# The first products of each SwiGLU stage on the tile of tokens that is ready first, the other tile's rows turned between them, and an MLP that waits for its hidden tiles in fours

## The chip, the cores and the metric

The kernel runs on one core of a Trainium2 chip. The metric is device time in microseconds of one execution, inputs and outputs in the chip's memory, all numbers fp32. Lower is better.

## What is computed

Two blocks of two layers each work on 256 tokens of width 1024. The first block (a diffusion-like block with attention, retention and an S5 scan) also has 256 context tokens in its first layer. What the change touches are its two MLPs and the four SwiGLU layers of the second block:

```python
def squared_relu_mlp(h, w1, w2):
    return jnp.square(jax.nn.relu(h @ w1)) @ w2

def swiglu(x, w_gate, w_up, w_down):
    return (jax.nn.silu(x @ w_gate) * (x @ w_up)) @ w_down

def second_block(x, ...):
    for l in range(DEPTH):
        x = layer_norm(ALPHA * x + 0.5 * swiglu(x, ffn1_w_gate[l], ffn1_w_up[l], ffn1_w_down[l]), ln1_g[l], ln1_b[l])
        y = hybrid_mixer(x, w_in[l], ...)
        x = layer_norm(ALPHA * x + y, ln2_g[l], ln2_b[l])
        x = layer_norm(ALPHA * x + 0.5 * swiglu(x, ffn2_w_gate[l], ffn2_w_up[l], ffn2_w_down[l]), ln3_g[l], ln3_b[l])
    return x
```

`w_gate` and `w_up` are 1024 x 2816, `w_down` 2816 x 1024.

## The kernel before

Each engine has its own program, written out by hand in the order in which it runs; the engines meet at semaphores. Tokens lie in tiles of 128 (t = 0 and 1; in MLP0, the first layer's MLP, also two context tiles). Weights are streamed by the SP queue into a ring of four slots; the load of a slot is released when TensorE has begun the weight tile after the one that was in it (`mm` with `T.first`), so the place of that matmul in TensorE's order sets when the load is issued.

**MLP0** (`tensor_mlp0`, `vector_mlp0`) goes over the hidden width in two halves. A half makes 16 hidden tiles f of 128 columns for 512 tokens on TensorE, VectorE squares the relu of each into `h1T` (L866, L868), then the second product runs for two column halves s, in four parts of four f each, over four token tiles. Between these products TensorE does pieces of the S5 preparation: transposes L2034 of the "ends" that VectorE has built (`ends_built`, its marker copy L2015) and the lags (L2049). VectorE computes S5 powers and levels behind f = 12 and f = 14. Ahead of the second product TensorE waits for `hidden_ready`, which VectorE raises by a marker copy (L887) after f = 15.

**A SwiGLU stage** (`tensor_ffn`, `scalar_ffn`, `vector_ffn`; stage n = 0 to 3) goes over w_gate and w_up in 11 groups ("units") of 256 columns. The product of two token tiles with gate and up over two halves of the depth is made in seven products of four matmuls instead of eight (a fast matrix scheme): products 0 and 1 are plain ones (tile 0 with the gate), the others take sums: `token_sum` (four, L2722, 512 columns) and `weight_sum` (four per unit, L2735, 1024 columns), all made by VectorE. VectorE adds the products up (L2767), ScalarE takes silu, VectorE multiplies (L2772), TensorE turns the hidden rows, ScalarE copies them. The down product (`tensor_seven`) has the same scheme for 768 columns; the last 256 columns are plain products, tile by tile (`tensor_last_columns`), 22 matmuls each (32 in the MLP of the second layer, MLP1).

**Between stages** each row tile gets its last sums (`vector_last_rows` after a SwiGLU stage: L2634; `vector_sum` after a mixer: L2823; L2873 and L2876 after MLP1), its norm (`vector_norm_tile`, L2840, with a root on ScalarE), is turned by TensorE (`tensor_turn_rows`, L2434, eight transposes) and copied with the norm's gain and shift to the columns `hT` (`drain_rows_turned`, on ScalarE L2452, on VectorE L2454). Only when both tiles' columns are there (`tensor_needs_hT`) does TensorE begin stage n, and VectorE its token sums and weight sums (`vector_ffn_sums`), followed by the rows for the next residual (`vector_next_rows`, L2849 to L2855: six operations). Stages 0 and 2 follow MLP1 and the layer before, where tile 0 is ready first; stages 1 and 3 follow a mixer, whose output product does tile 1 first. The mixers (`tensor_mixer2`) turn tile 0 first and begin with products on it.

## Time and profile before

| | |
|---|---|
| median of 3 runs | 2543.18 us (2539.36 to 2544.16) |
| the profiled execution, whole | 2542.72 us |
| its span in the profile | 2540.9 us |
| busy: TensorE, VectorE, ScalarE, GpSimd | 92%, 53%, 16%, 8% |
| mean granted clock of TensorE | 0.964 of 2.4 GHz |
| chain that ended last | PE 82%, DVE 11%, DMA 3%, ACT 2% |

The span is one profiled execution; the time of that execution contains 1.8 us around it. PE is TensorE, DVE VectorE, ACT ScalarE, POOL GpSimd, SPq the queue that loads weights. In a timeline a row merges instructions of one kind that follow one another, and its bracket gives the idle time of the engine in front of it and the instruction that ended it. Each fp32 matmul stands as two records.

### The profile page before, as it was taken

Reading aid. Unit: us, or ns where it says so; the run is one execution under the profiler, and the core shown is the slowest. Engines: PE = TensorE matmul, PEld = TensorE weight load, DVE = VectorE, ACT = ScalarE, POOL = GpSimd, SP = SyncE. Lnnn points to the kernel's source line nnn. Section 1 sums busy time; section 2 is a strip of 40 time slices with the busy share of each in tenths; the row PEclk is TensorE's granted clock in tenths of the full one; section 3 lists DMA queues with packets and bytes.
Section 4 is the critical chain, followed back from the end, with each engine's and each line's share of the span. In section 5 each row is a group of like instructions: output and inputs, shape, how many; then the busy total and the mean of one; then the engine's idle time right before and its main releaser. Section 6 shows DMA issues by size and latency. Waiting matters only on the chain.

```text
span 2540.9 us, 28736 instructions
## 1 busy us (share of the span) xinstructions
PE 2343.4 (92%) x11250; PEld 1553.0 (61%) x11250; DVE 1338.2 (53%) x2596; ACT 417.7 (16%) x913; POOL 205.5 (8%) x396
## 2 busy tenths in 40 slices
PE   7999989999999985499999999889999999889998
PEld 3445654444444433258768866557867886566885
DVE  2145563265566027424547763248766874255875
ACT  2122342000101013320001100131101110131110
POOL 1000000302555201000001000000000000000000
PEclk9999999999999997699999999899999999999999
DMA  7547612423444318245446554415555555514553
GB/s 244 190 151 240 202 49 66 102 66 108 149 150 149 124 58 291 101 132 152 154 158 219 167 159 143 126 47 164 171 161 159 170 164 161 147 50 141 170 162 124
DMA packets 278087, 371.10 MB, mean 146 GB/s; under 512 B 24838, under 2 KB 231169, under 8 KB 273217
## 3 DMA queue, kind: packets, MB, share of 16 engines
q1 hardware_dynamic: 260432, 332.30, 41.0%
q0 software_dynamic: 16752, 36.44, 4.6%
q8 instruction: 90, 1.47, 0.3%
q10 hardware_dynamic: 768, 0.53, 0.1%
q14 instruction: 45, 0.36, 0.0%
HBM read 345.10 MB, written 22.02 MB: 144 GB/s over the span
## 4 chain that ended last, share of the span: by engine, by line
PE 82%; DVE 11%; DMA 3%; ACT 2%; issue 1%; SPq 0%; POOL 0%; DVEq 0%; ACTq 0%; POOLq 0%
PE banks L222 72%; DMA weights<-in_w_in 1%; DMA weights<-in_ada_w 1%; PE banks L1338 1%; PE banks L1367 1%; DVE big L2735 1%; PE banks L2660 1%; PE banks L449 1%; PE banks L3257 1%; PE banks L3230 1%; PE banks L2034 0%; ACT h_columns L2452 0%; PE banks L1356 0%; DVE normed_rows L1632 0%; ACT normed_rows L3344 0%
## 5 line engine op out<-in xcount | busy, mean ns | idle before, releaser
L222 PE MATMUL banks<-weights,big 128*128 128x256 f32 (+4 forms) x2128 | 581.5, 445 | 70.1 <-ACT big L1036 51.0
L222 PE MATMUL banks<-weights,h_columns 128*128 128x256 f32 (+4 forms) x1664 | 544.1, 483 | 26.5 <-DVEq L2459 8.0
L222 PEld LDWEIGHTS banks<-weights,big 128*128 128x128 f32 (+2 forms) x2128 | 342.4, 187 | 272.7 <-issue 143.1
L222 PEld LDWEIGHTS banks<-weights,h_columns 128*128 128x128 f32 x1664 | 322.6, 196 | 221.8 <-issue 150.2
L222 PE MATMUL banks<-h_columns,weights 128*128 128x512 f32 (+1 forms) x1024 | 338.4, 491 | 4.2 <-ACTq L2459 2.4
L222 PEld LDWEIGHTS banks<-h_columns,weights 128*128 128x128 f32 x1024 | 195.2, 192 | 133.5 <-issue 117.1
L222 PE MATMUL banks<-big 128*128 128x256 f32 x1056 | 235.5, 379 | 2.2 <-DVE big L2735 2.2
L222 PEld LDWEIGHTS banks<-big 128*128 128x128 f32 x1056 | 200.3, 190 | 30.9 <-DVE big L2735 3.4
L2767 DVE TENSOR_TENSOR big<-banks,big 128x256 f32<-128x256 f32 x308 | 130.1, 422 | 85.1 <-PE banks L222 79.3
L2100 POOL DMA_DIRECT2D s_inside<-kernel_lags x256 | 127.4, 506 | 47.3 <-ACT statistics L2084 44.7
L2578 DVE TENSOR_TENSOR normed_rows<-weights 128x384 f32<-128x384 f32 x120 | 66.9, 558 | 101.0 <-PE banks L222 98.7
L222 PE MATMUL banks<-normed_rows,big 128*128 128x384 f32 (+1 forms) x368 | 115.6, 449 | 0.0
L2808 POOL DMA_DIRECT2D row_vectors<-in_ln_g x6 | 3.3, 544 | 1346.9 <-DVE statistics L2855 804.3
L2735 DVE TENSOR_TENSOR big<-weights 128x1024 f32<-128x1024 f32 x88 | 107.8, 1225 | 5.9 <-DMA weights<-in_ffn_w_up 3.0
L2735 DVE TENSOR_TENSOR big<-weights,big 128x1024 f32<-128x1024 f32 x88 | 107.8, 1225 | 3.0
L222 PEld LDWEIGHTS banks<-normed_rows,big 128*128 128x128 f32 (+1 forms) x368 | 59.4, 176 | 40.6 <-DVE normed_rows L2578 0.6
L222 PE MATMUL banks<-big,h_columns 128*128 128x256 f32 x352 | 83.3, 379 | 0.0
L721 DVE TENSOR_TENSOR normed_rows<-banks,row_vectors 128x512 f32<-128x512 f32 x16 | 11.1, 692 | 131.5 <-PE banks L222 131.3
L866 DVE TENSOR_SCALAR normed_rows<-banks 128x512 f32<-128x512 f32 x32 | 22.1, 691 | 101.5 <-PE banks L222 101.0
L1036 DVE COPY big<-banks 128x512 f32<-128x512 f32 (+5 forms) x50 | 31.4, 628 | 75.5 <-PE banks L222 64.5
L222 PE MATMUL banks<-weights,silu_c 128*32 128x256 f32 x768 | 52.1, 413 | 18.7 <-DMA weights<-in_ada_w 13.9
L2578 DVE TENSOR_TENSOR normed_rows<-weights,normed_rows 128x384 f32<-128x384 f32 x120 | 67.0, 558 | 4.2
(468 smaller groups left out, 2296.9 us busy)
## 6 DMA issues: line engine op xcount, KB each, us to landing
weights<-in_mlp_w SPq DMA_DIRECT2D x52, 1024.0 KB, 5.4
weights<-in_ada_w SPq DMA_DIRECT2D x48, 1024.0 KB, 7.3
weights<-in_ffn_w_gate SPq DMA_DIRECT2D x44, 1024.0 KB, 5.3
weights<-in_ffn_w_up SPq DMA_DIRECT2D x44, 1024.0 KB, 5.3
weights<-in_ffn_w_down SPq DMA_DIRECT2D x48, 768.0 KB, 4.3
weights<-in_w_out SPq DMA_DIRECT2D x12, 1024.0 KB, 5.0
weights<-in_mlp_w SPq DMA_DIRECT2D x16, 768.0 KB, 4.3
weights<-in_w_in SPq DMA_DIRECT2D x16, 768.0 KB, 4.5
```

The lines of the kernel that those rows point to most:

```text
L222: ins = T.engine.matmul(out, lhsT, rhs, start=start, stop=stop)
L449: ins = T.engine.matmul(self.ps[:, bank, 2 * j:2 * j + 2], self.ada_rows[:, n % 2 if buffer is None else buffer, j * P:(j + 1) * P], self. ...
L1036: return (lane.engine.copy if lane.name == "scalar" else lane.engine.tensor_copy)(out, in_)
L1338: ins = e.matmul(self.ps[:, n % 2, c0:TOK], self.qkT[0:QK, h % 2, 0, t * P:(t + 1) * P], self.qkT[0:QK, h % 2, 1, c0:TOK], start=True, sto ...
L1367: ins = e.matmul(self.ps[o:o + V_DIM, b, 0:P], self.kv[:, u, h, NOPE:NOPE + V_DIM], self.pT_of(m)[:, u * P:(u + 1) * P], start=u == keys[0 ...
L2100: e.dma_start(dst, src).then_inc(self.sem("inside_stored"), 16)
L2578: V.engine.tensor_tensor(out, in0, in1, ALU.subtract).then_inc(self.sem("down_sums"), 1)
L2660: ins = T.engine.transpose(self.ps[:, 7, f * N_LAT + t * P:f * N_LAT + (t + 1) * P], self.hidden_rows[:, t, f * P:(f + 1) * P], self.ident ...
L2735: V.engine.tensor_tensor(out, in0, in1, ALU.subtract).then_inc(self.sem("weight_sums"), 1)
L2767: e.tensor_tensor(out, self.ps[:, b, 0:256], other, ALU.add).then_inc(self.sem(name), 1)
L3230: ins = e.matmul(out, self.zT[:, h0 + j, t * P:(t + 1) * P], self.zT[:, 12 + g:16:2, 0:keys], start=True, stop=True)
L3257: ins = e.matmul(self.ps[:, 6 + m % 2, o:o + HD + 1], self.pT2[:, m % 2, j, 2 * c + u, :], self.v2[:, u, c, g, :], start=u == 0, stop=u == t)
```

## The change

- **MLP0.** The marker copy `hidden_ready` is gone. Each hidden tile raises `hidden_tiles`, and TensorE waits, in the first column half, for four more of them ahead of each of the four parts.
- **The turning of the first tile.** It stands inside the second tile's last product: after two of the weight tiles of `tensor_last_columns` (six matmuls of 22 are left, 16 of 32 in MLP1), or between the two column halves of the mixer's output product. The mixer's entry has it too.
- **The SwiGLU stage.** In stages 1 and 3 the roles of the tiles are swapped (`ffn_tile`), so that the plain products 0 and 1 of the first unit are on the tile turned first. They wait for that tile's columns alone (`first_columns`, raised by ScalarE). The other tile is turned behind product 0 (stages 0 and 2) or behind product 1 (stages 1 and 3).
- **VectorE.** The first unit's weight sums 0 and 1 stand ahead of the second tile's last sums instead of behind the token sums (`vector_first_weight_sums`); in stage 0 they lie in other memory. At the mixer's entry VectorE copies tile 0's turned half before it takes up tile 1.

```diff
@@ tensor_mlp1, tensor_mlp0
-        self.tensor_last_columns(T, self.mlp1_down())
+        self.tensor_last_columns(T, self.mlp1_down(), lambda: self.tensor_turn_rows(T, 0, 0, ("scalar", "scalar"), (1, 0)))
...
-            T.engine.wait_ge(self.sem("hidden_ready"), T.due("hidden_ready"))
             for s in range(2):
                 for part in range(4):
                     slot = self.tile_begins(T)
+                    if s == 0:
+                        T.engine.wait_ge(self.sem("hidden_tiles"), T.due("hidden_tiles", 4))
@@ vector_mlp0
-                V.engine.tensor_tensor(self.h1T[:, f, :], tmp, tmp, ALU.mult).then_inc(self.sem("vector_step"), 1)
+                V.engine.tensor_tensor(self.h1T[:, f, :], tmp, tmp, ALU.mult).then_inc(self.sem("hidden_tiles"), 1)
...
-            V.engine.tensor_copy(self.sm[:, 0:1], self.ident[:, 0:1]).then_inc(self.sem("hidden_ready"), 1)
-            V.engine.wait_ge(self.sem("hidden_ready"), V.due("hidden_ready"))
@@ tensor_last_columns
+                if t and c == 1 and between:
+                    between()
@@ tensor_ffn
+            if i == 0:
+                done("first_columns")
+                T.engine.wait_ge(*T.freed(0))
+                T.engine.wait_ge(*T.freed(1))
             T.first = True
             product(i, 0, "first_copied", lambda k: h(k, 0), lambda k: gate[:, k, :])
+            if i == 0 and n % 2 == 0:
+                turn_second()
             product(i, 1, "gate0_ready", lambda k: h(4 + k, 0), lambda k: gate[:, 4 + k, :])
             if i == 0:
+                if n % 2:
+                    turn_second()
+                self.tensor_needs_hT(T)
...
                 done("token_sums", 2)
@@ vector_ffn_sums and new
-        for j in range(2):
-            self.vector_token_sum(V, j)
-        for j in range(2):
-            self.vector_weight_sum(V, n, 0, j)
-        for j in range(2, 4):
-            self.vector_token_sum(V, j)
-            self.vector_weight_sum(V, n, 0, j)
+        for j in range(3):
+            self.vector_token_sum(V, n, j)
+        self.vector_weight_sum(V, n, 0, 2)
+        self.vector_token_sum(V, n, 3)
+        self.vector_weight_sum(V, n, 0, 3)
+
+    def vector_first_weight_sums(self, V, n):
+        for j in range(2):
             self.vector_weight_sum(V, n, 0, j)
@@ vector_to_mixer
-        self.vector_last_rows(V, 1)
         self.drain_rows_turned(V, 0, 1, 0, n)
         self.turned_by(V)
+        self.vector_last_rows(V, 1)
@@ vector_to_ffn
-        for s in range(2):
-            self.vector_sum(V, 0, s, 6 + s, 1.0)
+        self.vector_sum(V, 0, 0, 6, 1.0)
+        self.vector_first_weight_sums(V, 2 * (n - 2) + 1)
+        self.vector_sum(V, 0, 1, 7, 1.0)
@@ vector_to_next_layer (and the same in vector_first_rows)
+        self.vector_first_weight_sums(V, 2)
         self.vector_last_rows(V, 1)
@@ scalar_to_ffn (scalar_from_ffn alike)
         self.scalar_root(A, r[:, 1:2])
+        self.scalar_first_tile(A, 1, n)
         self.scalar_root(A, r[:, 0:1])
-        self.drain_rows_turned(A, 1, 0, 0, n)
-        self.drain_rows_turned(A, 1, 1, 0, n)
@@ project_out2
+            if s == 0 and between:
+                between()
```

How the instructions stand. TensorE at the entry of stage 1 (behind the first mixer), from the mixer's last output product to the first unit; L2434 are the transposes of the rows, "big" holds the token and weight sums. Before:

```order
L222 MATMUL banks<-weights,big 128x512 x16
L2434 MATMUL banks<-identity,x_rows 128x128 x16
L222 MATMUL banks<-weights,h_columns 128x256 x8
L222 MATMUL banks<-big 128x256 x12
L222 MATMUL banks<-big,h_columns 128x256 x4
```

and with the change (L2433 are the same transposes):

```order
L222 MATMUL banks<-weights,big 128x512 x8
L2433 MATMUL banks<-identity,x_rows 128x128 x8
L222 MATMUL banks<-weights,big 128x512 x8
L222 MATMUL banks<-weights,h_columns 128x256 x8
L2433 MATMUL banks<-identity,x_rows 128x128 x8
L222 MATMUL banks<-big 128x256 x12
```

One tile's transposes moved into the output product, the other's behind the first eight matmuls of the stage.

VectorE at the same entry, from tile 0's last half to the work on the next rows (L2849). Before:

```order
L2823 SCALAR_TENSOR_TENSOR x_rows<-banks,x_rows 128x512
L2826 BN_STATS statistics<-x_rows 128x6
L2835 BN_AGGR statistics<-statistics 128x2
L620 TENSOR_SCALAR statistics<-statistics 128x1
L623 RECIPROCAL statistics<-statistics 128x1
L2840 TENSOR_SCALAR x_rows<-x_rows,statistics 128x512 x2
L2454 TENSOR_SCALAR h_columns<-banks,norm_columns 128x128 x4
L2722 TENSOR_TENSOR big<-h_columns 128x512
L2722 TENSOR_TENSOR big<-big,h_columns 128x512
L2735 TENSOR_TENSOR big<-weights 128x1024
L2735 TENSOR_TENSOR big<-weights,big 128x1024
L2722 TENSOR_TENSOR big<-h_columns 128x512
```

and with the change (L2758 are the weight sums, L2848 the row sum, L2865 the norm, L2745 the token sums):

```order
L2758 TENSOR_TENSOR big<-weights 128x1024
L2758 TENSOR_TENSOR big<-weights,big 128x1024
L2848 SCALAR_TENSOR_TENSOR x_rows<-banks,x_rows 128x512
L2851 BN_STATS statistics<-x_rows 128x6
L2860 BN_AGGR statistics<-statistics 128x2
L620 TENSOR_SCALAR statistics<-statistics 128x1
L623 RECIPROCAL statistics<-statistics 128x1
L2865 TENSOR_SCALAR x_rows<-x_rows,statistics 128x512 x2
L2453 TENSOR_SCALAR h_columns<-banks,norm_columns 128x128 x4
L2745 TENSOR_TENSOR big<-h_columns 128x512
L2745 TENSOR_TENSOR big<-big,h_columns 128x512
L2745 TENSOR_TENSOR big<-h_columns 128x512
```

Two weight sums moved from behind the token sums to ahead of the tile's last row sum.

In MLP0 the order of the instructions stays; the one wait in front of the second product became four, one for each part, and the transposes' wait for `ends_built` stands behind the first part, as before.

## Rows read from the trace of the kernel before

**Rows 1.** Whole span: busy time of each engine (share) x instructions, from the page.

```profile
PE 2343.4 (92%) x11250; PEld 1553.0 (61%) x11250; DVE 1338.2 (53%) x2596; ACT 417.7 (16%) x913; POOL 205.5 (8%) x396
```

**Rows 2.** Waits of TensorE: engine, line, releaser: us in total, times, longest.

```profile
PE banks L222 <- DVE statistics L887: 10.2, 2, 8.1
PE banks L222 <- ACTq L2459: 9.7, 4, 2.9
...
PE banks L2434 <- DVE x_rows L2840: 6.2, 3, 2.2
```

**Rows 3.** Timeline, MLP0's first half: start, us, engine, line, what, count [idle before].

```profile
575.29 6.99 PE L222 MATMUL banks<-weights,big 128*128 128x512 f32 x10 [8.13 <-DVE statistics L887]
...
582.58 0.15 DVE L2015 COPY statistics<-identity 128x1 f32<-128x1 f32 x1
...
591.57 0.60 PE L2034 MATMUL banks<-identity,big 128*128 128x128 f32 x4
...
639.51 14.00 PE L222 MATMUL banks<-weights,big 128*128 128x512 f32 x32
```

**Rows 4.** Timeline, MLP0's second half, TensorE.

```profile
825.55 5.40 PE L222 MATMUL banks<-weights,big 128*128 128x512 f32 x8 [2.10 <-DVE statistics L887]
...
830.87 0.27 PE L2049 MATMUL banks<-aux,big 64*16 64x112 f32 x1
```

**Rows 5.** Stretches: busy us (x) of the engines, then granted clock, DMA share.

```profile
575.00:577.00 2.00, 1.71 (x2) 0.83 (x3) 1.93 (x4) 0.00 (x0) 0.00 (x0) 0.50 0.00 0
```

**Rows 6.** Timeline, entry of the first SwiGLU.

```profile
1332.62 0.37 SPq L312 DMA_DIRECT2D weights<-in_ffn_w_up  x1
...
1339.17 0.42 DVE L2873 TENSOR_TENSOR normed_rows<-banks,row_vectors 128x256 f32<-128x256 f32 x1 [12.93 <-PE banks L222]
...
1346.16 5.42 PE L222 MATMUL banks<-big 128*128 128x256 f32 x24
```

**Rows 7.** The page's row of the weight sums (busy, mean ns), its issue row (landing).

```profile
L2735 DVE TENSOR_TENSOR big<-weights 128x1024 f32<-128x1024 f32 x88 | 107.8, 1225 | 5.9 <-DMA weights<-in_ffn_w_up 3.0
...
weights<-in_ffn_w_up SPq DMA_DIRECT2D x44, 1024.0 KB, 5.3
```

**Rows 8.** Timeline, entry of the second mixer.

```profile
2152.17 1.04 PE L2434 MATMUL banks<-identity,x_rows 128*128 128x128 f32 x8
...
2155.00 5.40 PE L222 MATMUL banks<-weights,h_columns 128*128 128x384 f32 x16 [1.79 <-DVEq L2459]
```

**Rows 9.** Timeline, entry of the second SwiGLU.

```profile
1711.27 0.37 SPq L312 DMA_DIRECT2D weights<-in_ffn_w_up  x1
...
1717.35 0.69 DVE L2823 SCALAR_TENSOR_TENSOR x_rows<-banks,x_rows 128x512 f32<-128x512 f32 x1 [5.45 <-PE banks L222]
...
1720.35 1.97 PE L2434 MATMUL banks<-identity,x_rows 128*128 128x128 f32 x8 [2.23 <-DVE x_rows L2840]
...
1724.13 0.69 DVE L2722 TENSOR_TENSOR big<-h_columns 128x512 f32<-128x512 f32 x1 [0.34 <-ACTq L2459]
...
1724.47 6.68 PE L222 MATMUL banks<-weights,h_columns 128*128 128x256 f32 x16 [2.15 <-ACTq L2459]
...
1732.07 1.23 DVE L2849 TENSOR_TENSOR x_rows<-x_rows,row_vectors 128x1024 f32<-128x1024 f32 x1
...
1743.58 1.78 PE L222 MATMUL banks<-big 128*128 128x256 f32 x7 [0.35 <-DVE big L2735]
```

**Rows 10.** Timeline, entry of the third SwiGLU.

```profile
1929.45 0.37 SPq L312 DMA_DIRECT2D weights<-in_ffn_w_up  x1
...
1935.14 0.42 DVE L2634 SCALAR_TENSOR_TENSOR x_rows<-banks,x_rows 128x256 f32<-128x256 f32 x1 [6.45 <-PE banks L222]
...
1949.38 1.23 DVE L2849 TENSOR_TENSOR x_rows<-x_rows,row_vectors 128x1024 f32<-128x1024 f32 x1
...
1960.89 5.45 PE L222 MATMUL banks<-big 128*128 128x256 f32 x24 [1.46 <-DVE big L2735]
```

**Rows 11.** Timeline, entry of the S5 scan, TensorE.

```profile
955.54 5.39 PE L222 MATMUL banks<-weights,normed_rows 128*32 128x256 f32 x64 [10.29 <-DMA normed_rows<-h_columns]
```

More of the change, by code:

```diff
@@ L2638, in vector_last_rows, with ffn_tile, weight_sum_of, tensor_ffn @@
         V.engine.wait_ge(self.sem("vector_step"), V.due("vector_step"))
-    def tensor_ffn(self, T, n):
+    @staticmethod
+    def ffn_tile(n, t):
+        return 1 - t if n % 2 else t
+    def weight_sum_of(self, n, i, j):
+        if (n, i) == (0, 0) and j < 2:
+            return self.xn[:, 1024 * (j + 1):1024 * (j + 2)].rearrange("p (k n) -> p k n", k=4)
+        return self.weight_sum[:, j]
+    def tensor_ffn(self, T, n, turn_second, between):
         done = lambda name, count=1: T.engine.wait_ge(self.sem(name), T.due(name, count))
-        assert T.seen["hT_from_scalar"] == self.FFN_COLUMNS[n]
-        for b in range(BANKS):
-            T.engine.wait_ge(*T.freed(b))
         def product(i, b, taken, lhs, rhs):
@@ L2679, in tensor_ffn @@
             done("weight_sums")
-            product(i, 4, "third_ready", lambda k: ts[:, 2, k], lambda k: ws[:, 2, k])
+            product(i, 4, "third_ready", lambda k: ts[:, 2, k], lambda k: ws(2)[:, k])
             if i:
@@ L2684, in tensor_ffn @@
             T.first = True
-            product(i, 5, "gate1_ready", lambda k: h(4 + k, 1), lambda k: ws[:, 3, k])
+            product(i, 5, "gate1_ready", lambda k: h(4 + k, 1), lambda k: ws(3)[:, k])
             product(i, 6, "up0_ready", lambda k: ts[:, 3, k], lambda k: up[:, 4 + k, :])
@@ L2731, in vector_weight_sum @@
         gate, up = (self.ring[:, m % SLOTS, :].rearrange("p (k n) -> p k n", n=256) for m in (tile, tile + 1))
-        ws = self.weight_sum
-        out, in0, in1 = ((ws[:, 0], up[:, 0:4], gate[:, 0:4]), (ws[:, 1], up[:, 4:8], ws[:, 0]),
-                         (ws[:, 2], up[:, 4:8], up[:, 0:4]), (ws[:, 3], gate[:, 4:8], ws[:, 1]))[j]
+        ws = [self.weight_sum_of(n, i, m) for m in range(4)]
+        out, in0, in1 = ((ws[0], up[:, 0:4], gate[:, 0:4]), (ws[1], up[:, 4:8], ws[0]),
+                         (ws[2], up[:, 4:8], up[:, 0:4]), (ws[3], gate[:, 4:8], ws[1]))[j]
         V.engine.tensor_tensor(out, in0, in1, ALU.subtract).then_inc(self.sem("weight_sums"), 1)
@@ L2936, in vector_result, with scalar_first_tile @@
                 V.engine.wait_ge(self.sem("result_ready"), V.due("result_ready"))
+    def scalar_first_tile(self, A, t, n):
+        for half in range(2):
+            self.drain_rows_turned(A, t, half, 0, n)
+        A.engine.sem_inc(self.sem("first_columns"), 1)
     def scalar_from_ffn(self, A, n, mixer):
@@ L2943, in scalar_from_ffn @@
             self.turned_by(A)
+        else:
+            self.scalar_first_tile(A, 0, n)
         self.scalar_root(A, r[:, 1:2])
-        if not mixer:
-            self.drain_rows_turned(A, 0, 0, 0, n)
-            self.drain_rows_turned(A, 0, 1, 0, n)
         self.drain_rows_turned(A, 1, 0, 2, n)
@@ L3276, in turn_y2, with project_out2 @@
             T.hand([b], "scalar")
-    def project_out2(self, T, slots, t, bank):
+    def project_out2(self, T, slots, t, bank, between=None):
         T.engine.wait_ge(*T.freed(3))
```

49 lines of the change are left out of this document (23 added, 26 removed).

## The prediction

> **What bounds the kernel now.** The page comes first: TensorE is busy for 92% of the span [rows 1], so a change pays where TensorE stands idle or runs at its low clock, and costs where it adds to that. The list of TensorE's waits then says which idle time the change can reach. Five kinds are there: the wait for the marker copy L887 behind the hidden tiles, 10.2 us in two places; the waits for ScalarE's and VectorE's copies of turned rows (L2459), and for normalised rows (L2840), which together stand at the entries of the SwiGLU and mixer stages [rows 2]. Last the timeline, stage by stage, shows what such a wait costs beside its own length. After the 8.13 us in MLP0 ten records took 6.99 us [rows 3], where 32 of the same kind take 14.00, or 0.44 each; ten should take 4.4, so 2.6 us more were lost. The granted clock there was 0.50, the 1.2 GHz level, after TensorE had stood idle [rows 5]. (Each fp32 matmul stands as two records.)
>
> The sum is made against the profiled execution's own time, 2542.7 us; the median of the three runs is 0.5 us above it. About 0.2% (5.1 us) is what a measurement of this kernel can tell from no change.
>
> **MLP0, first half.** The product over the hidden tiles waited for all 16 of them; now its first quarter waits for four, which were ready long before. TensorE starts at 575.29 - 8.13 = 567.2 and the quarter takes 13.8 us (32 records, less the tail of the last), to 581.0. Right behind it stand the transposes L2034 of the S5 ends, and these wait for VectorE's marker L2015, which ends at 582.7 [rows 3]; VectorE is not freed earlier, except by the marker copy of 0.15 us that is gone. So a new wait of 1.6 us comes in, and the transposes start at 582.6 where they started at 591.57: **9.0 us gained**. The last quarter needs tile 16, ready by 575.3, some 40 us before it is asked for. The weight tiles are older loads of a queue that was idle then (DMA share 0.00 in [rows 5]), so I cost their wait at nothing. Bounds: the new wait may drop the clock, as the 8.13 us did, which takes 2.6 back.
>
> **MLP0, second half.** The wait was 2.10 us, and the eight records after it took until 830.87, 5.3 us, where eight at 0.44 take 3.5 [rows 4]. Nothing else is asked of VectorE there. Gain 2.1 + 1.9 = **4.0 us**.
>
> **Entries of the two mixers.** Tile 0 is turned inside tile 1's last product, before its last six matmuls. The eight records of the transposes cost the same 1.0 us, but the drains now run beside those matmuls (2.6 us at 0.22 a record) instead of in front of an idle TensorE. VectorE drains before it takes up tile 1, and no longer behind it. The mixer's first product began at 2155.00; with last columns and transposes over at 2152.17 + 1.04 = 2153.2 it begins there [rows 8]. **1.8 us each, 3.6 in all**; bounds 0 (the copies end later than the product) and 1.8. Its weight tiles were issued before the point of the transposes.
>
> **Entries of the second and fourth SwiGLU** (mixer to SwiGLU). Tile 1 is turned early, the two first products run on it, and the rows of tile 0 are turned behind them. But the first two weight sums now stand on VectorE ahead of tile 0's last half. They read the up tile, which was issued at 1711.27 [rows 9]; that load is released by a matmul behind the transposes now, 1.0 later, and lands 5.3 us after issue [rows 7]: 1717.6. Two sums at 1.23 [rows 7] end at 1720.1. Behind them is queued the sum L2823 that began at 1717.35, and behind that the norm, and TensorE's transposes wait for the norm: they move from 1720.35 to 1723.1. From the transposes to the token sums it was 3.8 us (1720.35 to 1724.13), 1.0 of it low clock (1.97 for eight records against 1.04 in [rows 8]); so the token sums start at 1723.1 + 2.8 = 1725.9. VectorE had eight sums from there to the next rows' work, 1724.13 to 1732.07; two are gone, 7.9 - 2.5 = 5.4 us, so that work starts at 1731.3, **0.8 us earlier**. This is what counts, since the second column group's third product at 1743.58 waited for VectorE (0.35 us) [rows 9]. TensorE itself would be ready sooner: its first product on token sums can start at 1725.9 + 1.4 = 1727.3 instead of 1731.2, 3.9 us. Of that 3.1 us will stand idle later. Hence 0.8 from below and 3.9 from above, and I take 0.8, by the row that shows VectorE as the releaser. Two such entries: **1.6 us**.
>
> Whether the clock falls matters less than it did. Before, idle stretches of 2.23 and 2.15 us were followed by sixteen records in 6.68 us, where they take 3.5 [rows 9]: 3.1 us lost. Now idle stretches of about 1.7 us (before tile 0's transposes) and 2.6 us (before the token sums) remain. I expect the low clock after the second, and its 3 us hidden in the wait for VectorE. The Trainium skill (TensorE: Matmul & The Clock Gate, "HAM oscillation — how this bites in real kernels") says that a matmul loop broken by waits starts each burst cold; by that rule the later wait would cost once more what the first did, and the sum would be 3.1 us worse at each entry. The trace agrees as to what one wait does.
>
> **Entry of the third SwiGLU** (layer to layer). The up tile was issued at 1929.45, ahead of the transposes, and lands at 1934.8; the sums end at 1937.3, and tile 1's sum starts then instead of at 1935.14. Rows ready 2.5 us later (3.0 in the case above, less two operations of 0.27), transposes at 1939.8, token sums at 1942.6, next rows' work at 1942.6 + 5.4 = 1948.0 against 1949.38 [rows 10]: **1.4 us**. VectorE held TensorE here too, for 1.46 us at 1960.89, so TensorE's own 3 us do not come through.
>
> **Entry of the first SwiGLU.** Up tile at 1332.62 + 1.0 + 5.3 = 1338.9; sums end at 1341.4, where L2873 started at 1339.17, so 2.2 us of the early start are lost. Rows at +0.9 (two operations of 0.42), transposes to 1343.3, copy 0.7, two token sums 1.4: the products on sums start at about 1345.6, against 1346.16 [rows 6]: **0.5 us**; from 0 to 1.5, the latter if the up tile lands in time.
>
> Sum: 9.0 + 4.0 + 3.6 + 1.6 + 1.4 + 0.5 = 20.1 us; 2542.7 - 20.1 = 2522.6, about 2523 against the median.
>
> **Rivals.**
> 1. The clock falls at the new waits and it is not hidden: 2.6 us in MLP0 and 3.1 at each of three SwiGLU entries, 11.9 in all at most, so 2526 to 2535, about 2530. For it: 2.10 us of idle time was enough in [rows 4]. Against it: 1.79 us was not, in [rows 8] (sixteen records of 384 columns in 5.40, 0.34 each), and the new wait of MLP0 is 1.6.
> 2. VectorE catches up and TensorE keeps its 3.9, 3.9 and 3.2 us: 7.6 more, 2515. Against it stand the two waits for L2735 in [rows 9, 10].
> 3. MLP0's 13.0 us are swallowed: the S5 scan starts behind a DMA wait of 10.29 us [rows 11], and if that waited for stores and not for rows turned just before, the start would stay where it is. Then 20.1 - 13.0 = 7.1, 2536. The scan's DMA reads rows that TensorE and the copies have just finished, so I think it moves along.
> 4. Slower than before: the split entries hold TensorE at 1.2 GHz through the first column groups. Product time at that clock is double, so each us of it costs half. It decides from (20.1 + 5.1) x 2 / 3, about 17 us of products at low clock beyond what is hidden, at each of three entries, more than one whole group; at 20 us each, 2542.7 - 20.1 + 30 = 2553. The Trainium skill (Perfetto Trace Analysis, "Matmul Optimizations") asks for matmuls back to back in batches, and this change splits them. Against it: behind a wait of 1.46 us in the second group 24 records took 5.45 us, 0.23 each [rows 10].
> 5. It does not do what it says: a bank or slot wait holds the first products where the old one did, and MLP0's quarter too: no change, 2543.
>
> **How the numbers follow.** Forecast 0.58 (its own range 2519 to 2526), rival 1 0.22, rival 2 0.08, rival 3 0.08, rivals 4 and 5 0.02 each. The predicted time is the forecast's. 2517 to 2533 leaves out rivals 2 to 5 and the tail of rival 1, together 0.2. Faster by over 0.2% are all but rivals 4 and 5: 0.96; the same 0.02; slower 0.02.
>
> **What would show it.** Right: no wait on the hidden tiles, and a wait of 1.6 us on L2034 near 581, then the transposes at about 582.6; all of MLP0's second half some 9 us earlier, what follows it 13 us; no wait at the mixers' first products; at the SwiGLU entries VectorE waiting for the up tile, TensorE waiting for rows for about 1.7 us, for token sums, and again about 2 us for L2735's successor in the second group. Wrong: granted clock 0.50 behind the new wait in MLP0 or in the second groups (rival 1), no VectorE wait there (rival 2), the scan's start unmoved (rival 3).

## The result and the profile after

| | before | changed |
|---|---|---|
| median | 2543.67 us of 4 runs (2539.36 to 2546.15) | 2523.2 us of 4 runs (2520.04 to 2525.72) |
| ratio | | 0.9921, 95% interval 0.9905 to 0.9936 |
| profiled execution; its span | 2542.7; 2540.9 us | 2524.4; 2522.6 us |

Faster by 20 us, 0.8%. The forecast was 2523.0 (2517 to 2533). The page of the changed kernel has the same number of matmuls as [rows 1], and TensorE busy with them for 4.8 us less:

```profile
PE 2338.6 (93%) x11250; PEld 1552.3 (62%) x11250; DVE 1338.3 (53%) x2594; ACT 417.7 (17%) x913; POOL 205.5 (8%) x396
```

TensorE's waits, as in [rows 2] (engine, line, releaser: us in total, times, longest). Lines have moved: L2745 is now a token sum, L2758 a weight sum (L2735 before), L2865 the norm, L2014 the marker of the S5 sums.

```profile
PE banks L222 <- DVE big L2745: 9.0, 4, 3.3
...
PE banks L2433 <- DVE x_rows L2865: 4.6, 3, 1.8
PE banks L222 <- DVE big L2758: 4.1, 3, 2.4
...
PE banks L2033 <- DVE statistics L2014: 1.7, 1, 1.7
```

The marker behind the hidden tiles (10.2 us in two waits) is gone. What stands there now is what the prediction named: the S5 marker, rows, token sums, and the weight sum in the second group.

The timeline of MLP0's first half, then TensorE's row at the end of the second half, answer to [rows 3, 4]; and the granted clock in the new wait and behind it, to [rows 5]:

```profile
580.87 0.15 DVE L2014 COPY statistics<-identity 128x1 f32<-128x1 f32 x1
...
581.08 0.66 PE L2033 MATMUL banks<-identity,big 128*128 128x128 f32 x4 [1.72 <-DVE statistics L2014]
```

```profile
812.87 3.60 PE L222 MATMUL banks<-weights,big 128*128 128x512 f32 x8
816.40 0.27 PE L2048 MATMUL banks<-aux,big 64*16 64x112 f32 x1
```

```profile
579.00:581.00 2.00, 0.36 (x1) 0.00 (x0) 1.93 (x3) 0.00 (x0) 0.00 (x0) 1.00 0.00 0
581.00:583.00 2.00, 1.92 (x8) 1.21 (x9) 1.97 (x3) 0.58 (x1) 0.00 (x0) 1.00 0.00 0
```

The transposes wait 1.72 us (forecast 1.6) and the clock stays at 1.00, the 2.4 GHz level. In the second half the eight records take 3.60 us, not 5.40, without a wait.

The second mixer's entry [rows 8] and the S5 scan's [rows 11]:

```profile
2130.07 1.04 PE L2433 MATMUL banks<-identity,x_rows 128*128 128x128 f32 x8
...
2133.54 5.32 PE L222 MATMUL banks<-weights,h_columns 128*128 128x384 f32 x16
```

```profile
940.88 4.97 PE L222 MATMUL banks<-weights,normed_rows 128*32 128x256 f32 x64 [9.56 <-DMA normed_rows<-h_columns]
```

The mixer's product has no wait in front of it. The scan has moved from 955.54 to 940.88 with its DMA wait still in front of it.

The second SwiGLU's entry [rows 9], VectorE and TensorE, and the page's row of the weight sums [rows 7]:

```profile
1698.11 1.23 DVE L2758 TENSOR_TENSOR big<-weights 128x1024 f32<-128x1024 f32 x1 [5.56 <-DMA weights<-in_ffn_w_up]
...
1700.63 0.69 DVE L2848 SCALAR_TENSOR_TENSOR x_rows<-banks,x_rows 128x512 f32<-128x512 f32 x1
...
1703.62 1.24 PE L2433 MATMUL banks<-identity,x_rows 128*128 128x128 f32 x8 [1.40 <-DVE x_rows L2865]
...
1706.48 0.69 DVE L2745 TENSOR_TENSOR big<-h_columns 128x512 f32<-128x512 f32 x1
...
1708.15 7.11 PE L222 MATMUL banks<-big 128*128 128x256 f32 x24 [3.29 <-DVE big L2745]
...
1711.91 1.23 DVE L2874 TENSOR_TENSOR x_rows<-x_rows,row_vectors 128x1024 f32<-128x1024 f32 x1
```

```profile
L2758 DVE TENSOR_TENSOR big<-weights 128x1024 f32<-128x1024 f32 x87 | 106.6, 1225 | 23.3 <-DMA weights<-in_ffn_w_up 20.5
```

Add the 19.35 us by which TensorE was early when this entry began, and the forecast's times stand there: sum L2848 at 1719.98 (forecast 1720.1), transposes 1722.97 (1723.1), token sums 1725.83 (1725.9), next rows' work 1731.26 (1731.3). VectorE's wait for up tiles in this row is 20.5 us, where it was 3.0; 17.4 us of it stand at the second to fourth entry (5.56, 6.33 and 5.53). The first entry's sums lie in other memory and so in another row, with a wait of 12.56 us; there VectorE had waited as long before, for TensorE (12.93 in [rows 6]).

**Where the 18.4 us between the two spans came from.** The same matmul's start in both traces, subtracted, gives by how much TensorE is early; below is how that number grew from one place to the next. The kernels of the experiments stand in the same table, always against the first profile of before (us).

| kernel | start to 465 | MLP0 1st | 2nd | 831 to 1118 | to 1351, 1st SwiGLU | mixer 1 entry | to 1703 | 2nd SwiGLU | 3rd | mixer 2 entry | to 2299 | 4th |
|---|---|---|---|---|---|---|---|---|---|---|---|---|
| forecast | 0 | 9.0 | 4.0 | 0 | 0.5 | 1.8 | 0 | 0.8 | 1.4 | 1.8 | 0 | 0.8 |
| changed | 1.5 | 8.95 | 3.98 | 1.8 | 0.25 | 1.94 | 0.9 | 0.81 | -0.65 | 1.95 | -3.9 | 0.84 |
| e1 MLP0 only | 4.9 | 8.94 | 3.97 | 2.2 | -0.01 | 0.00 | -0.1 | -0.01 | -0.01 | 0.00 | -3.7 | -1.69 |
| e2 entries only | 3.2 | -0.03 | -0.01 | 1.2 | 0.03 | 1.95 | 0.3 | 0.70 | -0.44 | 1.95 | -3.6 | 0.74 |
| e3 mixers back | 5.3 | 8.96 | 3.98 | 2.4 | 0.24 | -0.01 | 0.6 | 0.72 | 1.12 | -0.01 | -3.7 | 0.77 |
| e4 changed again | 2.5 | 8.95 | 3.98 | 2.2 | 0.32 | 1.95 | 0.8 | 0.57 | -0.41 | 1.95 | -3.9 | 0.65 |
| e9 before again | 0.3 | -0.01 | -0.06 | 4.2 | -0.01 | -0.01 | -0.3 | 0.00 | 0.00 | -0.01 | -3.6 | -0.01 |
| e5 sums back | 3.3 | 8.94 | 4.00 | 1.9 | -1.48 | 1.95 | 0.3 | 0.05 | 0.04 | 1.95 | -3.5 | 0.04 |
| e6 release first | 5.5 | 8.93 | 3.97 | 1.2 | 1.08 | 1.95 | 0.5 | 1.73 | 1.34 | 1.95 | -3.9 | 1.56 |
| e7 levels later | 3.5 | 10.83 | 4.06 | 2.4 | 0.23 | 1.95 | 4.1 | 0.65 | -0.41 | 1.95 | -5.1 | 0.72 |
| e8 rows spread | 5.4 | 8.94 | 3.98 | 2.3 | -0.11 | 1.95 | 0.5 | 2.34 | 4.34 | 1.96 | -3.6 | 1.51 |
| e10 three edits | 0.4 | 10.82 | 4.06 | 3.0 | 0.93 | 1.95 | 0.1 | 2.99 | 4.32 | 1.94 | -5.7 | 3.07 |
| e11 old entries, spread | 2.5 | 8.95 | 3.99 | 2.2 | -0.30 | 0.01 | 0.7 | 1.35 | 1.80 | -0.01 | -4.4 | 2.03 |
| e12 norm first | 5.6 | 10.83 | 4.06 | 3.3 | 1.04 | 1.95 | 0.4 | 2.37 | 2.36 | 1.95 | -3.4 | 2.49 |

The columns that hold a part of the change repeat to a tenth of a us or two, wherever the clock does not fall. Those that hold none (start, 831 to 1118, and the insides of the two mixers, "to 1703" and "to 2299") differ by 4 to 6 us between executions. Every row is one profile.

### The profile page after: what moved, and what is told of

It is laid out like the page before. It is cut to its first block, busy times and chain, and to the rows that moved or that the text cites. A ratio compares the mean times of both kernels' runs of the same rounds, so it can differ in the third digit from the quotient of the medians.

```text
span 2522.6 us, 28741 instructions
## 1 busy us (share of the span) xinstructions
PE 2338.6 (93%) x11250; PEld 1552.3 (62%) x11250; DVE 1338.3 (53%) x2594; ACT 417.7 (17%) x913; POOL 205.5 (8%) x396
## 4 chain that ended last, share of the span: by engine, by line
PE 81%; DVE 11%; DMA 4%; ACT 2%; issue 1%; SPq 0%; POOL 0%; DVEq 0%; ACTq 0%; POOLq 0%
PE banks L222 71%; DMA weights<-in_w_in 1%; DMA weights<-in_ada_w 1%; PE banks L1337 1%; PE banks L1366 1%; DVE big L2758 1%; DMA weights<-in_ffn_w_up 1%; PE banks L2670 1%; PE banks L3261 1%; PE banks L2033 1%; PE banks L3288 1%; PE banks L449 1%; PE banks L1355 0%; PE banks L2433 0%; ACT normed_rows L3377 0%
## 5 line engine op out<-in xcount | busy, mean ns | idle before, releaser
L222 PE MATMUL banks<-weights,h_columns 128*128 128x256 f32 (+4 forms) x1664 | 538.2, 479 | 14.4 <-issue 6.6
L222 PE MATMUL banks<-normed_rows,big 128*128 128x384 f32 (+2 forms) x384 | 119.3, 447 | 0.9 <-DVE big L2745 0.8
L2758 DVE TENSOR_TENSOR big<-weights 128x1024 f32<-128x1024 f32 x87 | 106.6, 1225 | 23.3 <-DMA weights<-in_ffn_w_up 20.5
L2758 DVE TENSOR_TENSOR big<-weights,big 128x1024 f32<-128x1024 f32 x86 | 105.3, 1225 | 3.0
L721 DVE TENSOR_TENSOR normed_rows<-banks,row_vectors 128x512 f32<-128x512 f32 x16 | 11.1, 692 | 127.6 <-PE banks L222 127.4
L222 PEld LDWEIGHTS banks<-big,h_columns 128*128 128x128 f32 x352 | 63.8, 191 | 7.0
```

The lines of the kernel that those rows point to most:

```text
L222: ins = T.engine.matmul(out, lhsT, rhs, start=start, stop=stop)
L2758: V.engine.tensor_tensor(out, in0, in1, ALU.subtract).then_inc(self.sem("weight_sums"), 1)
```

## The experiments

Theory: the terms of the prediction's sum, each at its place, with VectorE's queue as what limits the SwiGLU entries. Rivals: the entries are limited by TensorE's turning or by the up tile, or the clock takes the gain back. Each was run against the kernel before on the same chip. The changed kernel itself was measured beside e1 to e3 alone, as e4; e5 to e8 and e9 to e12 ran on two other chips, and "by the ratios" sets their ratios to before against its 0.9925. Of e5 to e8 no interval is clear of its 0.9907 to 0.9943, so what one of these edits is worth rests on the places in the table.

**e1 and e2: the change in two halves.** e1 has, in the kernel before, the MLP0 edit alone:

```diff
-            T.engine.wait_ge(self.sem("hidden_ready"), T.due("hidden_ready"))
...
                     slot = self.tile_begins(T)
+                    if s == 0:
+                        T.engine.wait_ge(self.sem("hidden_tiles"), T.due("hidden_tiles", 4))
```

e2 has the rest: the changed kernel with these lines undone.

> The kernel before with the MLP0 part of the change alone: the second products wait for four hidden tiles. My theory: the terms of MLP0 stand by themselves, 9.0 us in the first half (a wait of about 1.7 us for VectorE's marker left in front of the transposes of the S5 ends) and 4.0 us in the second, so 13 us below the kernel before, about 2530.5, and the first product of the first SwiGLU entry 13 to 15 us earlier. The trace of the changed kernel showed 1.6 us more between MLP0 and the S5 scan than my sum has: if that belongs to this part it is 14.6 us, about 2529; if it is chance it is gone here. Rival (the entries carry more than their terms, MLP0 less): under 10 us.

> The changed kernel with MLP0 as before (the second products wait for all 16 hidden tiles): only the mixer and SwiGLU entries are changed. My theory: the parts add up, so 20 us less 13 to 14.6 is left, 5 to 7 us below the kernel before, 2536 to 2538, and 13 to 15 us above the changed kernel. Rival (entries are worth nothing, or pay only when MLP0 has moved): no more than 3 us below the kernel before.

Measured: e1 2528.1 us, ratio 0.9943 (0.9928 to 0.9959); e2 2535.3 us, 0.9974 (0.9963 to 0.9985). In thousandths of 2541 us that is 5.7 + 2.6 = 8.3 (21 us), and the changed kernel has 7.9 and 7.5 in its two measurements: the halves add up. At its place e1 gives 12.91 us (the changed kernel 12.93) and nothing at the entries but for a spell of low clock at the last; e2 gives nothing in MLP0 and 4.9 us at the entries (changed 5.1). The 1.6 us that I had placed between MLP0 and the S5 scan lie elsewhere: 1.5 of the 14.66 us at the scan stand before 465 already, and 1.6 more come behind the scan's start, by 1118. Both are chance, as e2 and e9, without this part, have such pieces too.

**e3: the mixers' turning back.**

```diff
-                            lambda: self.tensor_turn_rows(T, 0, 0, ("scalar", "vector")))
+                            None)
...
         e = T.engine
+        self.tensor_turn_rows(T, 0, 0, ("scalar", "vector"))
```

and VectorE drains behind its last rows again.

> The changed kernel with the turning of tile 0 at the two mixer entries put back behind the last product, and VectorE draining behind its last norm again. My theory: each entry gives back the 1.8 us predicted (2.0 us in the trace), so 4 us above the changed kernel, about 2527, and TensorE waits 1.8 us for normalised rows and copies again. But 3.1 us were lost inside the second mixer where TensorE, waiting for nothing new, ran 16 products of 408 columns at its low clock; rival: that loss belongs to the early turning, then undoing it costs only about 1 us at the second mixer, or nothing.

Measured 2525.1 us, 0.9936 (0.9917 to 0.9954): 0.0011, or 2.8 us, above the changed kernel's 0.9925 of the same chip, within both intervals. The places say more than the medians: the entry's 1.95 us are gone (-0.01 both times), and the wait is back:

```profile
1531.40 5.40 PE L222 MATMUL banks<-weights,h_columns 128*128 128x384 f32 x16 [1.79 <-DVEq L2458]
```

The loss inside the second mixer (2155 to 2299) is there without the early turning, 3.7 us, so the rival's reading of it falls.

**e4: the changed kernel again; e9: the kernel before again.**

> The changed kernel once more, on the same chip as the three others, as what they are compared with: 2523 us, 0.992 of the kernel before. Its profile is a second look at the places where the clock fell in the first: if the low clock in the second group of the third SwiGLU entry (behind a wait of 2.36 us) and inside the second mixer stand here too, they belong to the kernel; if they are gone, a single trace's clock is chance of about 2 to 3 us at each.

> The kernel before once more, with a profile of its own: a ratio of 1.000, and a second look at two stretches in which every later kernel differed from the first profile of before without any part of the change in them. Between the last ends of MLP0 (830.87) and the S5 output (1118.36) all were 1.2 to 3.0 us shorter; in the second mixer, at the thin products of 15 and 30 columns and the 256-column products behind them, all but one were 2.8 to 3.7 us longer. My theory (the clock's phase at a wait or a thin product varies from execution to execution, and the first profile of before had luck in the second mixer): this profile is about 3 us longer there than the first. Rival (the shift by 13 to 20 us or the changed entries cause it): both stretches are as in the first profile, within 0.3 us.

Measured: e4 2523.5 us, 0.9925 (0.9907 to 0.9943). e9 2541.3 us, 1.0003 (0.999 to 1.0015), and its second profile settles the two open stretches: it is 4.2 us shorter than the first between 831 and 1118, and 3.6 us longer in the second mixer, with no edit at all. The timeline of that stretch, first profile of before, then e9, and the stretch of each (busy us of the five engines, granted clock, DMA):

```profile
2229.99 3.64 PE L3165 MATMUL banks<-aux,big 96*128 96x15 f32 x32
2233.49 3.70 PE L222 MATMUL banks<-weights,h_columns 128*128 128x256 f32 x16
```

```profile
2230.00:2237.20 7.20, 7.19 (x50) 6.42 (x48) 2.67 (x9) 3.98 (x6) 0.00 (x0) 1.00 0.20 67
```

```profile
2226.16 4.60 PE L3165 MATMUL banks<-aux,big 96*128 96x15 f32 x32
2230.59 6.09 PE L222 MATMUL banks<-weights,h_columns 128*128 128x256 f32 x16
```

```profile
2226.20:2236.80 10.60, 10.48 (x50) 9.02 (x48) 3.04 (x9) 4.02 (x7) 0.00 (x0) 0.68 0.17 46
```

Same instructions, no idle time between them: 7.2 us at clock 1.00, 10.5 us at 0.68. The first profile of before had the upper clock there; of the changed kernel's two, neither did. The 3.9 us that the changed kernel loses inside this mixer are not all here, though: 1.4 stand ahead of this stretch (2200 to 2229 of before), 1.7 in it and about 1.0 behind it (2285 to 2290), and e2, without the MLP0 part, has them at the same places. So e9 shows that a loss of this size needs no edit, not where each part of it comes from.

**e5: the first weight sums back behind the token sums.**

```diff
-        self.vector_first_weight_sums(V, 2 * (n - 2) + 1)
         self.vector_sum(V, 0, 1, 7, 1.0)
...
-        for j in range(3):
+        for j in range(2):
             self.vector_token_sum(V, n, j)
-        self.vector_weight_sum(V, n, 0, 2)
-        self.vector_token_sum(V, n, 3)
-        self.vector_weight_sum(V, n, 0, 3)
+        for j in range(2):
+            self.vector_weight_sum(V, n, 0, j)
+        for j in range(2, 4):
+            self.vector_token_sum(V, n, j)
+            self.vector_weight_sum(V, n, 0, j)
```

> The changed kernel with the first weight sums back behind the token sums at all four SwiGLU entries (the early turning of the tile that is ready first stays). My theory: VectorE's queue sets the second group. Without the sums in front, the last norm and the token sums come earlier, but two more sums of 1.23 us stand behind them, so the next rows' work and the second group's third product come 0.8 us later in the second and fourth entry, 0 to 1.4 in the third: 2 to 3 us above the changed kernel, and VectorE's 20 us of waiting for the up tile shrink to about 6. The clock adds up to 1.7 us either way at each entry. Rival (putting sums ahead of the up tile's landing costs more than it saves): 1 to 4 us below the changed kernel.

Measured 2525.4 us, 0.9935 (0.9917 to 0.9953), 2.5 us above the changed kernel by the ratios. TensorE in the second entry, and the page's row of the weight sums:

```profile
1709.28 7.56 PE L222 MATMUL banks<-big 128*128 128x256 f32 x24 [5.70 <-DVE big L2758]
```

```profile
L2758 DVE TENSOR_TENSOR big<-weights 128x1024 f32<-128x1024 f32 x87 | 106.6, 1226 | 8.0 <-DMA weights<-in_ffn_w_up 5.1
```

VectorE's wait for up tiles falls from 20.5 to 5.1 us, and the kernel is not faster: putting other work into that idle time gained nothing, as the two sums then stand behind it. The second and fourth entry are worth 0.05 and 0.04 us in place of 0.81 and 0.84. So the early turning gains there only together with the two sums ahead. The third has 0.04, against -0.65 in the changed kernel with its low clock and 1.12 in e3 without. The first entry turns from 0.25 to -1.48, more than I had expected for it: TensorE's first product on sums, which waited 0.82 us for the token sums, now waits for a weight sum:

```profile
1329.55 3.69 PE L222 MATMUL banks<-normed_rows,big 128*128 128x256 f32 x16 [3.23 <-DVE normed_rows L2758]
```

**e6: the turning behind the release of the next weight tile.**

```diff
                 for k in range(k0, k1):
                     ins = self.mm(T, self.ps[:, b, 0:width], down.rows(k, t), w[:, k - k0, :], k == 0, k == n_k - 1)
-                if t and c == 1 and between:
-                    between()
+                    if t and c == 2 and k == k0 and between:
+                        between()
```

and likewise in the output product of the mixer.

> The changed kernel with the turning inside the other tile's last product moved one matmul later, behind the one that releases the next weight tile's slot: at the first, second and fourth SwiGLU entry the up tile is issued 1.0 us earlier. My theory (VectorE waits for that tile, then holds TensorE): everything on VectorE comes 1.0 us earlier at three entries, 2 to 3 us below the changed kernel, and TensorE's waits for the sum L2745 shrink from 3.3 to 2.3 us. Rival (the sums wait for something else, or the third group's end is set by TensorE): no difference.

Measured 2517.8 us, 0.9909 (0.9892 to 0.9925): 0.0016, or 4 us, below the changed kernel. First, second and fourth entry 1.08, 1.73 and 1.56 against 0.25, 0.81 and 0.84: 0.7 to 0.9 us each, where I had expected 1.0. The third, which I had not counted in, has 1.34, mostly because the clock stayed up there this time, as in e3 with 1.12 (below). This also says what VectorE's wait for the up tile is worth: with the tile 1.0 us earlier (5.56 us of waiting at the second entry become 4.63) most of that comes through. One number of mine was wrong: the wait for L2745 stays 3.29, since turning, copies and sums follow each other at a fixed distance; what shrinks is the wait for rows in front of it, 1.37 to 0.65:

```profile
2295.38 1.24 PE L2433 MATMUL banks<-identity,x_rows 128*128 128x128 f32 x8 [0.65 <-DVE x_rows L2865]
...
2299.91 0.76 PE L222 MATMUL banks<-big 128*128 128x256 f32 x1 [3.29 <-DVE big L2745]
```

**e7: the S5 levels behind the first ends.**

```diff
-                if half == 0 and f == 14:
-                    self.vector_s5_levels(V)
...
                     self.vector_s5_from_state(V, gb)
+                    if gb == 0:
+                        self.vector_s5_levels(V)
```

> The changed kernel with VectorE's S5 levels moved from inside the product over hidden tiles to behind the first ends of MLP0, so that the marker which TensorE's transposes wait for is not behind them. My theory: the new wait of 1.72 us in front of the transposes is gone and nothing takes its place, 1.7 us below the changed kernel at that place, the clock there stays at its upper level as it does now. Rival (VectorE is late at the next point instead, at the levels' first reader): no gain, a wait of 1 to 2 us in front of the S5 products of this half.

Measured 2519.4 us, 0.9917 (0.99 to 0.9933), 2 us below the changed kernel by the ratios. VectorE's marker now stands 3 us ahead of the transposes, which wait for nothing, and the first half gives 10.83 in place of 8.95, the second its 4.06; no new wait stands in front of the S5 products:

```profile
574.26 0.15 DVE L2014 COPY statistics<-identity 128x1 f32<-128x1 f32 x1
...
577.22 0.60 PE L2033 MATMUL banks<-identity,big 128*128 128x128 f32 x4
```

**e8 and e11: the next rows' work spread**, with the new entries and with the old (e11 is e1 with this edit).

```diff
         self.vector_ffn_sums(V, 2 * (n - 2) + 1)
-        self.vector_next_rows(V, (1, 0))
...
             add(self.ups2[:, 0], 6, self.fourth, "up0_ready")
             hide(0)
+            if i and steps:
+                steps.pop(0)()
```

where each step is one of the six operations, or the marker.

> The changed kernel with the work on the next rows (six operations and a marker on VectorE) taken out of the space behind the first sums and put one operation behind each later pair of sums, in the second to fourth SwiGLU. My theory: TensorE's waits in the second group (1.3, 2.4 and 0.5 us, with 1.7 us of low clock behind the second) belong to that work, and the waits for L2745 in the first group do not: 4 to 6 us below the changed kernel, up to 10 if the 3.1 us that TensorE gains at each entry come through whole. Rival (the late up tile, not this work, is what VectorE is behind with): 1 us or less, the waits come back a group later. Second rival (the clock takes it back): the waits go, and products of 24 records take 7.1 us in place of 5.4 elsewhere.

> The kernel before with the MLP0 part and with the work on the next rows spread, but with the mixer and SwiGLU entries as before: the fourth corner beside the first, fourth and eighth run. My theory (that work holds TensorE only where TensorE is early): here it frees just the waits for L2734 in the second group, 0.4 to 1.9 us each and a spell of low clock, so 3 to 5 us below the first run (0.9943 to about 0.993), and the early entries are worth 8 to 10 us on top of it (to 0.9896) where they are worth 4.6 without it. Rival (spreading is worth the same 7 us with either entry): 0.9915.

Measured: e8 2514.0 us, 0.9896 (0.9878 to 0.9915), 7 us below the changed kernel by the ratios. e11 2524.3 us, 0.9926 (0.991 to 0.9941), 4.3 us below e1. The same stretch of the third entry, before this edit (changed kernel) and with it (e8):

```profile
1939.70 7.13 PE L222 MATMUL banks<-big 128*128 128x256 f32 x24 [2.36 <-DVE big L2758]
```

```profile
1919.21 5.42 PE L222 MATMUL banks<-big 128*128 128x256 f32 x24 [1.56 <-DVE big L2745]
...
1931.37 5.34 PE L222 MATMUL banks<-big 128*128 128x256 f32 x24
```

The wait of 2.36 us in the second group is gone, the first group's of 1.56 stays. The three entries give 2.34, 4.34 and 1.51 (changed: 0.81, -0.65, 0.84), 7.2 us more, which is the whole of the 7. Of these, 1.7 are the spell of low clock at the third entry, which e3 and e6 did not have either; 5.5 are the edit's alone. The up tile's lateness (rival) was therefore not what made the second group wait. With the old entries the edit gives 5.2 us at its three places, and by the ratios the new entries are worth 7.6 us on top of it, 3.9 of them the mixers', where without it they are worth 4.6: 3 us more, where I expected 3.4 to 5.4. The four ratios are each known to 4 or 5 us only, and the places do not bear it out: there the new entries give 12.0 - 4.9 = 7.1 us on top of the spread work (e8, e11) and 5.1 without it, and the changed kernel's spell of 1.7 us is nearly all of the difference. That the two edits help each other is not shown.

**e10 and e12: together.** e10 has the edits of e6, e7 and e8. e12 differs from it in where the first two weight sums stand:

```diff
-        self.vector_first_weight_sums(V, 2 * (n - 2) + 1)
         self.vector_sum(V, 0, 1, 7, 1.0)
         self.vector_norm_tile(V, 0, "rows_normed")
+        self.vector_weight_sum(V, 2 * (n - 2) + 1, 0, 0)
         self.drain_rows_turned(V, 0, 1, 2, n)
         self.turned_by(V)
+        self.vector_weight_sum(V, 2 * (n - 2) + 1, 0, 1)
```

> The changed kernel with the three edits that were faster alone: turning behind the release of the next weight tile, the S5 levels later, and the work on the next rows spread. Their ratios against the kernel before were 0.9909, 0.9917 and 0.9896 where the changed kernel had 0.9925. My theory (they act at different places and add up: about 4, 2 and 7 us): 0.9872, about 13 us below the changed kernel, 2509. Rival (the first and the third both cure VectorE's lateness, so together they are worth no more than the third): 0.9888, about 2513.

> The tenth kernel with the two first weight sums of the second to fourth SwiGLU behind the last tile's norm, one in the time in which TensorE turns that tile and one behind VectorE's drains. With the next rows' work spread, VectorE no longer sets the second group, and the norm comes 2.5 us earlier, the token sums 1 to 2 us, so about 1 us at each of three entries: 2 to 3 us below the tenth kernel. Rival (the drains and then the token sums wait behind a sum of 1.23 us, and the up tile's landing decides anyway): the same as the tenth within 1 us, or slower.

Measured: e10 2513.0 us, 0.9884 (0.9868 to 0.9901); e12 2511.1 us, 0.9874 (0.9857 to 0.9892). Both intervals lie below the changed kernel's 0.9925 (0.9907 to 0.9943), and they do not tell the two apart. The places do: e10's four entries give 0.93, 2.99, 4.32 and 3.07, e12's 1.04, 2.37, 2.36 and 2.49, so e12's order is 3.2 us worse where it differs at all (second to fourth). Its span is shorter since it was 5.6 us ahead of before at 465 and e10 0.4, with nothing changed up to there, and since it lost 3.4 us inside the second mixer and e10 5.7. So the places bear out the rival's expectation for e12, though the medians, 1.9 us apart, look like mine. TensorE's first product on sums, e10 then e12, in the second entry (both views end inside this product):

```profile
1705.59 2.68 PE L222 MATMUL banks<-big 128*128 128x256 f32 x7 [3.29 <-DVE big L2745]
```

```profile
1700.35 2.04 PE L222 MATMUL banks<-big 128*128 128x256 f32 x4 [5.03 <-DVE big L2745]
```

It starts 8.89 us (1705.59 - 1696.70) behind the entry's first products in e10 and 9.52 (1700.35 - 1690.83) in e12: the rows are turned earlier, but a sum of 1.23 us stands between the drains and the token sums. At the third entry the same shift makes a wait of 1.56 us one of 3.30, and the clock falls behind it: the 24 records take 7.10 us there in e12 and 5.42 in e10.

Now e10, on its places against e8 (+1.9 in MLP0, +1.0, +0.65, 0 and +1.6 at the entries), should be 5 us better than e8; the ratios show 3, with overlapping intervals. Its 0.9884 is nearer to the rival's 0.9888 than to my 0.9872. The places speak for the theory: e6's edit gives 3.2 us at the entries on top of e8, and 2.5 alone (first, second and fourth). Both are the fastest kernels of this study, 10 and 13 us below the changed one by the ratios.

## Why the prediction was right, and where not

- **MLP0, both halves.** 9.0 and 4.0 were predicted, 8.95 and 3.98 measured, and the same within 0.02 in every kernel with that part unaltered. The bound, that the new wait would drop the clock, did not come about in any: 1.72 us at clock 1.00. e7 shows that it was a wait for VectorE's S5 work and nothing else. (The low clock had cost 2.4 us behind the old wait, 16.43 us for all 32 records against 14.00, and not 2.6; the 9.0, taken between two starts, do not rest on it.)
- **Mixer entries.** 1.8 predicted, 1.94 and 1.95 measured. The last columns and transposes were over 0.15 us sooner than the 2153.2 of the forecast.
- **Second and fourth SwiGLU.** 0.8 predicted, 0.81 and 0.84 measured (0.57 and 0.65 in e4), through VectorE's row of times that stands above. TensorE's two idle stretches were 1.40 and 3.29 us, not 1.7 and 2.6. Taking VectorE as the bound and not TensorE's 3.9 us was the choice that mattered; e8 shows it, since there the second entry gives 2.34. Rival 2 (VectorE catches up) is out: the wait in the second group stands at all three places. (Its price was summed wrongly: 3.9 + 3.9 + 3.2 is 8.0 us over the 3.0 of the forecast, not 7.6.)
- **Third SwiGLU: the step that failed.** "1.4 us" was measured as -0.65. Of that step the times of VectorE held but for 0.3 us, by which the up tile was later than taken (next rows' work at 1928.18 + 20.16 = 1948.34 against 1948.0), and TensorE's product in the second group was 1.03 us earlier in place of 1.4. But TensorE had waited 2.36 us for it, and the clock fell, which the step's sum puts at nothing and leaves to rival 1. VectorE's row, then the granted clock of the product's stretch (TensorE busy, clock, DMA), in the changed kernel and in e3 behind the same wait:

```profile
1928.18 1.23 DVE L2874 TENSOR_TENSOR x_rows<-x_rows,row_vectors 128x1024 f32<-128x1024 f32 x1
```

```profile
1939.70:1943.20 3.50, 3.50 (x10) 0.58 0.74 234
```

```profile
1937.50:1940.20 2.70, 2.65 (x12) 1.00 0.85 264
```

  The 24 records took 7.13 us in the one and 5.45 in the other. That is rival 1, which I had priced at "3.1 at each of three SwiGLU entries": it was 1.7, and at one. Of six kernels with this entry and this wait of 2.35 or 2.36 us (changed, e2, e3, e4, e6, e7), four lost the 1.7, and e3 and e6 did not; their entries gave 1.12 and 1.34, close to the 1.4.
- **First SwiGLU.** 0.5 predicted, 0.25 measured: VectorE's first weight sum stood where it was forecast (1322.54 + 16.27 = 1338.81, against 1338.9), the products on sums at 1329.63 + 16.27 = 1345.90 and not 1345.6.
- **What was hidden.** In the first group of the second and fourth entry the clock did fall, 7.11 and 7.89 us for 24 records behind the waits of 3.29, and it cost nothing, as forecast, only that it was 1.7 to 2.4 us and not 3: the second group waited the less for it.
- **Rival 3** (MLP0's gain swallowed at the scan): out. The scan started 14.66 us earlier (1.5 of them from before 465), still behind 9.56 us of DMA. **Rival 4** (split entries hold TensorE at the low clock, slower than before): 1.7 us at one entry is far from its 17 us at each of three. **Rival 5**: out, by the absent waits.
- **The Trainium skill's rule** (TensorE: Matmul & The Clock Gate, "HAM oscillation — how this bites in real kernels", that a loop broken by waits starts each burst cold) was weighed at 3.1 us more per entry. The page tells it of a loop with longer waits than those of the second groups here. The traces agree for the first group of the second and fourth entry, and in the second group for one place and some executions. Behind the waits of 1.26 us in the second group of the second entry and 1.57 in the first group of the third, 24 records took 5.45 and 5.42.
- **The sum.** The terms at their places give 18.1 us against 20.1. Start-up, S5 stretch and the mixers' insides happened to add 0.3 to that between these two profiles, out of parts of +1.5, +1.8, +0.9 and -3.9, that e9 shows to be chance. The median's 20.5 us is thus right by mechanism, and to the last 2 us by luck.

## What to carry to other kernels

When a queue is late (here VectorE's), time that another engine gains comes through only up to the next place where it asks that queue for something; look for work in that queue that nobody waits for soon, and move it away. By the places that was worth 5.2 us with the old entries (e11) and 7.2 with the new (e8, 1.7 of them clock), at three places; making the other engine start earlier was worth 5.1 at six, 3.9 of them at the mixers. An order in which that queue idles less is not the better one for it: e5 took VectorE's wait from 20.5 to 5.1 us and lost 0.8 us at each of two entries, since the sums then stood in the way later. Ending the idle time sooner does gain (e6, 0.7 to 0.9 us for a tile 1.0 us earlier). And where edits are worth a us or two, compare the same instruction's start in two traces place by place: such differences repeated to 0.1 us or so, while medians of the kernel before differed by up to 2.6 us (2541.0 to 2543.7) and its single executions by 15 (2535.3 to 2550.1).

## What the runs showed of the hardware that was not expected

- The clock behind one and the same wait differs from execution to execution: 2.36 us of idle TensorE was followed by 24 records in 7.13 us or in 5.45. A wait of 1.89 us in e1's fourth entry was followed by 7.13, one of 1.84 in e9's second by 5.45; the wait of 2.10 in [rows 4] by eight records in 5.40 each time it was there (before, e2, e9). Nor does the length alone decide above that: behind waits of 3.29 or 3.30 us in the first groups 24 records took 6.9 to 8.4 us in all 17 cases, but behind the 3.23 us of e5's first entry 5.42 us, at clock 1.00.
- The clock also fell with no idle time in front, in and behind the mixers' 32 thin matmuls of 15 columns. From the first of these to the product L3178 (its line in before), the next but one behind them, it took one of three times in all mixers: 7.7 us (the second mixer of the first profile of before, the first of e7), 9.4 (among others the second of changed, e2, e4 and e6) or 11.0 to 11.1 (most). The steps are 1.65 to 1.7 us, the same as between 5.45 and 7.13: one spell of low clock or two. No kernel here tried to avoid these spells. That these matmuls cause them is argued from where the spells stand, not shown.
- Start-up and the S5 stretch, with DMA waits in both, vary by 5 and 4 us between executions of kernels that are identical there; this and the clock's spells are what the medians scatter by.
